# A norm's factors applied with tokens on partitions, and one recurrence's gates a slot sooner, in a two-block transformer kernel

## The reference, cut to what matters

```python
o = einsum('bhts,bhsv->bhtv', A, v)                          # 128 values per head and token
o = o * rsqrt(mean(o * o, axis=-1) + EPS) * norm_w           # a mean per head and token
o = o * silu(r)                                              # the gate
```

## Time and profile before

| | |
|---|---|
| median of 3 runs | 1113.66 us (1113.42 to 1113.71) |
| the profiled execution's own time | 1113.65 us |
| its span, first to last instruction | 1111.8 us |
| what lies around the span | 1.85 us |
| PE busy | 1097.7 us, 99% of the span |
| DVE busy, ACT busy | 750.7 us (68%), 608.6 us (55%) |
| mean granted TensorE clock | 0.998 of full speed |

### The profile page before, as it was taken

One profiled execution on the slowest core, in us unless ns is written; L12 is line 12 of the kernel. 1 busy time (PEld: TensorE's weight loads), 2 busy tenths in 40 slices (PEclk: granted clock), 3 DMA queues, 4 the chain that ended last, 5 costly groups with the idle time before them and its releaser, 6 DMA issues.

```text
span 1111.8 us, 22817 instructions
## 1 busy us (share of the span) xinstructions
PE 1097.7 (99%) x9532; PEld 1050.8 (95%) x9532; DVE 750.7 (68%) x980; ACT 608.6 (55%) x790; POOL 0.2 (0%) x4
## 2 busy tenths in 40 slices
PE   9999999999999999999999999999999999999997
PEld 8899999989999998999999999999999989999997
DVE  6355576677555555689969676866558657777776
ACT  6455456346444444687665555566555446545554
POOL 0000000000000000000000000000000000000000
PEclk9999999999999999999999999999999999999999
DMA  8433344564555555344434443444444545555451
GB/s 308 177 134 139 119 169 169 177 221 146 187 190 189 189 189 182 121 152 153 167 127 140 153 150 141 152 152 152 161 180 152 190 152 174 191 187 189 186 189 39
DMA packets 27113, 184.42 MB, mean 166 GB/s; under 512 B 3080, under 2 KB 3608, under 8 KB 5400
## 3 DMA queue, kind: packets, MB, share of 16 engines
q1 hardware_dynamic: 26456, 181.38, 45.6%
q10 hardware_dynamic: 576, 1.85, 0.5%
HBM read 182.17 MB, written 1.05 MB: 165 GB/s over the span
## 4 chain that ended last, share of the span: by engine, by line
PE 53%; DVE 1%; ACT 1%; issue 1%; ACTq 0%
PE pp L306 41%; PE pm L1733 2%; PE pm L1734 2%; PE pm L1735 2%; PE pm L919 1%; PE pm L389 1%; PE pm L387 1%; PE pm L388 1%; PE pm L1574 1%; PE pm L780 1%; PE pm L787 0%; PE pm L1349 0%; PE pm L1381 0%; DVE P L1067 0%; DVE wlo L288 0%
## 5 line engine op out<-in xcount | busy, mean ns | idle before, releaser
L288 DVE TENSOR_TENSOR wlo<-raw,whi 128x2048 fp32r<-128x2048 f32 x169 | 386.7, 2291 | 188.1 <-ACT whi L281 184.1
L306 PE MATMUL pp<-XH,whi 128*128 128x256 f32 x1696 | 485.5, 286 | 0.9 <-DVE wlo L288 0.5
L306 PE MATMUL pp<-XH,wlo 128*128 128x256 f32 x1696 | 481.3, 284 | 0.0
L306 PE MATMUL pp<-XL,whi 128*128 128x256 f32 x1696 | 481.3, 284 | 0.0
L281 ACT ACTIVATE whi<-raw 128x2048 fp32r<-128x2048 f32 x169 | 322.0, 1909 | 57.1 <-PE pp L306 33.8
L306 PEld LDWEIGHTS pp<-XH,whi 128*128 128x128 f32 x1696 | 326.0, 192 | 5.8 <-issue 2.4
L306 PEld LDWEIGHTS pp<-XL,whi 128*128 128x128 f32 x1696 | 326.1, 192 | 0.7
L306 PEld LDWEIGHTS pp<-XH,wlo 128*128 128x128 f32 x1696 | 326.1, 192 | 0.0
L1787 ACT ACTIVATE Y<-P 128x256 fp32r<-128x256 f32 x44 | 18.4, 418 | 132.6 <-DVE P L1820 132.6
L306 PE MATMUL pp<-Y,whi 128*128 128x256 f32 x480 | 86.9, 283 | 0.0
L306 PEld LDWEIGHTS pp<-Y,whi 128*128 128x128 f32 x480 | 75.2, 192 | 0.0
(11 more groups left out here) (321 smaller groups left out, 1300.1 us busy)
## 6 DMA issues: line engine op xcount, KB each, us to landing
raw<-stream SPq DMA_DIRECT2D x169, 1024.0 KB, 4.8
P<-gains ACTq DMA_DIRECT2D x3, 512.0 KB, 3.8
X<-xt SPq DMA_DIRECT2D x2, 512.0 KB, 4.3
raw<-stream SPq DMA_DIRECT2D x2, 512.0 KB, 6.7
out<-P SPq DMA_DIRECT2D x4, 256.0 KB, 2.3
C<-consts SPq DMA_DIRECT2D x1, 345.5 KB, 11.5
P<-rows_w ACTq DMA_DIRECT2D x1, 272.0 KB, 3.4
U<-poolw SPq DMA_DIRECT2D x1, 256.0 KB, 10.5
```

What stands on the lines that cost most here:

```text
L288: dve.tensor_tensor(wlo[:, slot, :], raw[:, slot, :], whi[:, slot, :].bitcast(F32), ALU.subtract).then_inc(lo_ready, 1)
L306: done = pe.matmul(dst, a, b, start=first and n == 0, stop=last and n == 2, **kw)
```

## The change

The outputs are made with the scores as the stationary operand, so tokens lie on partitions and each head's 128 channels along the row. The sum of squares is then a reduction along the row on DVE, and the eight factors are a column each, multiplied in by DVE while it takes `o` out of PSUM. Eight transposes on PE turn the scaled outputs back to channels on partitions, and one DVE instruction multiplies them by gain and gate. The `token_sum` and `spread_columns` matmuls, ACT's copy of `o` and the rounding of the columns go. PE has its two slots together (`st.go(2)`), ahead of the transposes. Besides, DVE's gates of r = 0 are queued one slot sooner.

```diff
 # gated_pe
-        o = [pm[:, 1024 + h * 256:1280 + h * 256] for h in range(4)]
+        o = [[pm[:, 1024 + u * 512 + h * 128:1152 + u * 512 + h * 128] for h in range(4)] for u in range(2)]
         for h in range(4):
-            pe.matmul(o[h][:, 128:256], g["v"](0, h), a_words(g, h)[:, 128:256], start=h % 2 == 0, ...)
+            pe.matmul(o[1][h], a_words(g, h)[:, 128:256], g["v"](0, h), start=h == 0, ...)
...
-        st.go(1)
-        pe.wait_ge(S("gated_squares"), r + 1)
+        st.go(2)
+        pe.wait_ge(S("gated_o_scaled"), r + 1)
         for h in range(4):
             for u in range(2):
-                i = token_sum(pe, bank(2)[:, 2 * h + u:2 * h + u + 1], HF[:, 4 + h, :], u)
-        i.then_inc(S("gated_sums"), 1)
-        st.go(1)
-        pe.wait_ge(S("gated_rsqrt"), r + 1)
-        pe.wait_ge(S("ident_rounded"), 1)
-        for h in range(4):
-            i = spread_columns(pe, bank(3 + h // 2)[:, (h % 2) * 256:(h % 2) * 256 + 256], (2 * h, 2 * h + 1))
-        i.then_inc(S("gated_norm_spread"), 1)
+                i = pe.transpose(bank(3 + h // 2)[:, (h % 2) * 256 + u * 128:(h % 2) * 256 + u * 128 + 128],
+                                 words(g["o"], u * 512 + h * 128, 128), ident)
+        i.then_inc(S("gated_o_turned"), 1)
 # gated_act
-        act.activation(P[:, g["o"]:g["o"] + 4, :], pm[:, 1024:2048]..., ACT.Copy).then_inc(S("gated_o_copied"), 1)
         act.activation(HF[:, 4:8, :], pm[:, 1024:2048]..., ACT.Square).then_inc(S("gated_squares"), 1)
...
-        act.activation(SC[:, 72:80], bank(2)[:, 0:8], ACT.Sqrt, bias=eps4, scale=4.0 / 128)
+        act.activation(SC[:, 72:80], SC[:, 72:80], ACT.Sqrt, bias=eps4, scale=4.0 / 128)
...
-            act.wait_ge(S("gated_rsqrt"), 3)
+            act.wait_ge(S("gated_o_scaled"), 3)
 # gated_dve
-        link(dve, dve.scalar_tensor_tensor(GD(g), GD(g), 1.0, P[:, g["r"]:g["r"] + 4, :], ALU.add, ALU.mult))
-        dve.wait_ge(S("gated_o_copied"), r + 1)
-        o = P[:, g["o"]:g["o"] + 4, :]
-        link(dve, dve.scalar_tensor_tensor(o, o, col(g["gain"]), GD(g), ALU.mult, ALU.mult))
+        gate, o = P[:, g["r"]:g["r"] + 4, :], P[:, g["o"]:g["o"] + 4, :]
+        link(dve, dve.scalar_tensor_tensor(gate, GD(g), 1.0, gate, ALU.add, ALU.mult))
         if r == 1:
             differences(0, gated(2))
+        by_head = lambda ap: ap.rearrange("p (n d) -> p n d", n=8)
+        dve.wait_ge(S("gated_squares"), r + 1)
+        dve.tensor_reduce(SC[:, 72:80], by_head(HF[:, 4:8, :]...), AX.X, ALU.add).then_inc(S("gated_sums"), 1)
         st.go(1)
         dve.wait_ge(S("gated_rms"), r + 1)
         link(dve, dve.reciprocal(SC[:, 80:88], SC[:, 72:80]))
-        round_columns(dve, SC[:, 80:88]).then_inc(S("gated_rsqrt"), 1)
+        dve.tensor_tensor(by_head(words(g["o"], 0, 1024)), by_head(pm[:, 1024:2048]),
+                          SC[:, 80:88].unsqueeze(2).to_broadcast([128, 8, 128]), ALU.mult).then_inc(S("gated_o_scaled"), 1)
         st.go(1)
...
-        dve.wait_ge(S("gated_norm_spread"), r + 1)
-        dve.tensor_tensor(o, o, pm[:, 1536:2560]..., ALU.mult).then_inc(S("gated_y_ready"), 1)
+        dve.wait_ge(S("gated_o_turned"), r + 1)
+        dve.scalar_tensor_tensor(o, pm[:, 1536:2560]..., col(g["gain"]), gate, ALU.mult, ALU.mult)
 # VectorE's queue, first stage
         gate_lo(dve, G1W[:, :], KT * 16, 1)
-        st.go(4)
+        st.go(3)
         gated_gates_dve(dve, 0)
         st.go(1)
         gated_decay_dve(dve, 0, slice(0, 2))
```

More of the change, by code:

```diff
@@ L925, in gated_pe @@
         wait_evac(pe, VALUES[r])
-        o = [pm[:, 1024 + h * 256:1280 + h * 256] for h in range(4)]
+        o = [[pm[:, 1024 + u * 512 + h * 128:1152 + u * 512 + h * 128] for h in range(4)] for u in range(2)]
         for h in range(4):
-            pe.matmul(o[h][:, 128:256], g["v"](0, h), a_words(g, h)[:, 128:256], start=h % 2 == 0, stop=False, skip_group_check=True)
+            pe.matmul(o[1][h], a_words(g, h)[:, 128:256], g["v"](0, h), start=h == 0, stop=False, skip_group_check=True)
         taken_scores(pe, r, 3)
@@ L931, in gated_pe @@
         for h in range(4):
-            pe.matmul(o[h][:, 0:128], g["v"](0, h), a_words(g, h)[:, 0:128], start=False, stop=True, skip_group_check=True)
-            i = pe.matmul(o[h][:, 128:256], g["v"](1, h), a_words(g, h)[:, 256:384], start=False, stop=True, skip_group_check=True)
+            pe.matmul(o[0][h], a_words(g, h)[:, 0:128], g["v"](0, h), start=h == 0, stop=True, skip_group_check=True)
+            i = pe.matmul(o[1][h], a_words(g, h)[:, 256:384], g["v"](1, h), start=False, stop=True, skip_group_check=True)
         i.then_inc(S("gated_o_ready"), 1)
-        st.go(1)
-        pe.wait_ge(S("gated_squares"), r + 1)
+        st.go(2)
+        pe.wait_ge(S("gated_o_scaled"), r + 1)
         for h in range(4):
             for u in range(2):
-                i = token_sum(pe, bank(2)[:, 2 * h + u:2 * h + u + 1], HF[:, 4 + h, :], u)
-        i.then_inc(S("gated_sums"), 1)
-        st.go(1)
-        pe.wait_ge(S("gated_rsqrt"), r + 1)
-        pe.wait_ge(S("ident_rounded"), 1)
-        for h in range(4):
-            i = spread_columns(pe, bank(3 + h // 2)[:, (h % 2) * 256:(h % 2) * 256 + 256], (2 * h, 2 * h + 1))
-        i.then_inc(S("gated_norm_spread"), 1)
+                i = pe.transpose(bank(3 + h // 2)[:, (h % 2) * 256 + u * 128:(h % 2) * 256 + u * 128 + 128],
+                                 words(g["o"], u * 512 + h * 128, 128), ident)
+        i.then_inc(S("gated_o_turned"), 1)
     def gated_logits_act(act):
@@ L1016, in gated_act @@
         act.wait_ge(S("gated_o_ready"), r + 1)
-        act.activation(P[:, g["o"]:g["o"] + 4, :], pm[:, 1024:2048].rearrange("p (a t) -> p a t", a=4), ACT.Copy)\
-           .then_inc(S("gated_o_copied"), 1)
         act.activation(HF[:, 4:8, :], pm[:, 1024:2048].rearrange("p (a t) -> p a t", a=4), ACT.Square)\
@@ L1023, in gated_act @@
         act.wait_ge(S("gated_sums"), r + 1)
-        act.activation(SC[:, 72:80], bank(2)[:, 0:8], ACT.Sqrt, bias=eps4, scale=4.0 / 128).then_inc(S("gated_rms"), 1)
+        act.activation(SC[:, 72:80], SC[:, 72:80], ACT.Sqrt, bias=eps4, scale=4.0 / 128).then_inc(S("gated_rms"), 1)
         st.go(1)
@@ L1129, in gated_dve @@
         dve.wait_ge(S("gated_r_tanh"), r + 1)
-        link(dve, dve.scalar_tensor_tensor(GD(g), GD(g), 1.0, P[:, g["r"]:g["r"] + 4, :], ALU.add, ALU.mult))
-        dve.wait_ge(S("gated_o_copied"), r + 1)
-        o = P[:, g["o"]:g["o"] + 4, :]
-        link(dve, dve.scalar_tensor_tensor(o, o, col(g["gain"]), GD(g), ALU.mult, ALU.mult))
+        gate, o = P[:, g["r"]:g["r"] + 4, :], P[:, g["o"]:g["o"] + 4, :]
+        link(dve, dve.scalar_tensor_tensor(gate, GD(g), 1.0, gate, ALU.add, ALU.mult))
         if r == 1:
             differences(0, gated(2))
+        by_head = lambda ap: ap.rearrange("p (n d) -> p n d", n=8)
+        dve.wait_ge(S("gated_squares"), r + 1)
+        dve.tensor_reduce(SC[:, 72:80], by_head(HF[:, 4:8, :].rearrange("p a t -> p (a t)")), AX.X, ALU.add).then_inc(S("gated_sums"), 1)
         st.go(1)
@@ L1139, in gated_dve @@
         link(dve, dve.reciprocal(SC[:, 80:88], SC[:, 72:80]))
-        round_columns(dve, SC[:, 80:88]).then_inc(S("gated_rsqrt"), 1)
+        dve.tensor_tensor(by_head(words(g["o"], 0, 1024)), by_head(pm[:, 1024:2048]), SC[:, 80:88].unsqueeze(2).to_broadcast([128, 8, 128]),
+                          ALU.mult).then_inc(S("gated_o_scaled"), 1)
         st.go(1)
@@ L1146, in gated_dve @@
                 dve.scalar_tensor_tensor(x, HF[:, 4 * b:4 * b + 4, :], 1.0, x, ALU.add, ALU.mult).then_inc(S("lm_silu"), 1)
-        dve.wait_ge(S("gated_norm_spread"), r + 1)
-        dve.tensor_tensor(o, o, pm[:, 1536:2560].rearrange("p (a t) -> p a t", a=4), ALU.mult).then_inc(S("gated_y_ready"), 1)
+        dve.wait_ge(S("gated_o_turned"), r + 1)
+        dve.scalar_tensor_tensor(o, pm[:, 1536:2560].rearrange("p (a t) -> p a t", a=4), col(g["gain"]), gate, ALU.mult, ALU.mult)\
+           .then_inc(S("gated_y_ready"), 1)
         if r != 1:
```

## The result

| | before | changed |
|---|---|---|
| median, first timing | 1113.66 us | 1102.82 us (1102.72 to 1102.86, 4 executions) |
| span of the profiled execution | 1111.8 us | 1101.0 us |
| ratio to the kernel before | | 0.9903, 95% interval 0.9886 to 0.9920 |

The changed kernel is 10.84 us faster; 11.4 were forecast (1102.3 us, range 1101.0 to 1104.8). The page of the changed kernel has the same balance as before: PE loses 72 matmuls and 10.6 us of busy time, and stays at 99%.

A forecast was written before the change was run, and what follows sets the result against it. PE, busy 99% of the span, was taken as the bound, so only its shorter queue or fewer waits help: 3.9 + 2.7 + 2.7 + 2.1 = 11.4 us off, forecast 1102.3 us, range 1101.0 to 1104.8.

The forecast's parts named there:

- gates a slot sooner: wait and clock: First scores of r = 0: PE's 2.45 us wait goes and 1.4 us of slow matmuls come back, 3.9 us.
- r = 0, PE's work behind the outputs: Sums and spreading go, eight transposes come: 9.37 us becomes one slot of 5.76 plus 0.93, gain 2.7 us.
- r = 1: Same pattern and durations behind the outputs of r = 1 as at r = 0: another 2.7 us.
- r = 2, limited by the chain on ACT and DVE: Ahead of L1363 the evacuation behind DVE's last multiplication holds PE some 0.9 us: gain 2.1 us instead of 2.7.
- the clock: First scores and levels of r = 0: without the pause no cause for the clock to fall, 1.4 us back.
- The upper end of 1.7: Highest price of each group of eight transposes, if each costs a two-part float32 matmul; gain at r = 0 then 1.9 us.
- No wait for DVE: Ahead of the transposes: scaled outputs ready 4.6 us before PE asks, 3.3 at the least; rival that they wait, 3%.
- The chain at r = 2: L281 starts near 636.15, 7.15 us to the gatings' end, last multiplication 643.3, next PE stage 649.4: gain 2.1 us.

The follow-up runs named there:

- the gates alone: The kernel before with only DVE's gates of r = 0 queued a slot sooner, old norm kept: 1109.48 us median over 7 executions.
- the norm alone: The changed kernel with the gates of r = 0 back in their old place: 1106.78, 1106.77, 1105.45 and 1105.28 us.
- the evacuation first: The changed kernel with, at r = 2, the last slot's evacuation queued ahead of the norm's last multiplication on ACT and DVE: 1101.36 us, again 1101.40.
- the run with four reductions: The changed kernel with DVE's reduction made four times in each recurrence: 1105.00, 1104.94, 1103.50 and 1103.43 us.
- one slot ahead of the transposes: The changed kernel with the transposes one slot sooner, one of PE's two slots ahead of them and one behind: 1105.32 us.

## Why the prediction was right, step by step

| step | forecast | measured |
|---|---|---|
| gates a slot sooner: wait and clock | 3.9 us | 4.0 by the gates alone (against the upper level); 4.0 from the traces |
| r = 0, PE's work behind the outputs | 2.7 | 2.64 |
| r = 1 | 2.7 | 2.62 |
| r = 2, limited by the chain on ACT and DVE | 2.1 | 1.78 |
| start of the kernel | none | 0.27 lost |
| sum | 11.4 | 10.8 |

The traces' values are distances between the same points. For the gates it is the start of the first level's matmuls, 61.96 before and 58.24 after: 3.72 sooner, although the first slot starts 0.27 later, so 4.0.

```profile
61.96 0.71 PE L908 MATMUL pm<-HF 64*128 64x128 f32 x8
```

```profile
58.24 0.71 PE L908 MATMUL pm<-HF 64*128 64x128 f32 x8
```

At r = 0 it is the distance from L1017 or L1012 to the attention's first matmul. At r = 1 and r = 2 it is the one from the first L932, among the outputs, to what follows the slots and the norm: the scores of r = 2 (L919), and `mlstm_pe`. Before, then after:

```profile
555.71 0.46 PE L932 MATMUL pm<-U,P 128*128 128x128 f32 x2 [0.42 <-ACT U L1014]
...
572.67 0.76 PE L919 MATMUL pm<-P,U 128*32 128x32 f32 x64
...
628.39 0.46 PE L932 MATMUL pm<-U,P 128*128 128x128 f32 x2 [0.42 <-ACT U L1014]
```

```profile
549.22 0.46 PE L932 MATMUL pm<-P,U 128*128 128x128 f32 x2 [0.42 <-ACT U L1009]
...
563.56 0.76 PE L919 MATMUL pm<-P,U 128*32 128x32 f32 x64
...
619.28 0.46 PE L932 MATMUL pm<-P,U 128*128 128x128 f32 x2 [0.42 <-ACT U L1009]
```

That is 16.96 and 14.34 us at r = 1, and with `mlstm_pe` at 651.48 and 640.59, 23.09 and 21.31 at r = 2. All of them sum to 10.8, the difference of the spans.

**The gates.** Every time in the chain came out within 0.3 us of the forecast, with the later start: decays done at 48.8 (48.6 forecast), first scores without a wait. The step that the prediction took as certain and that is not is the clock: a stretch at 0.50 follows the wait in most executions of the kernel before, not in all. The forecast was made against a median that lies on the upper level, so the sum held. The changed kernel's time does not depend on this, but the gain does: against the lower level it is some 9.3 us. That all four executions of the kernel before in the first timing lay on the upper level, as 9 of the 26 later ones did not, is luck.

**PE's work.** From the first transpose to what follows the eight it is 0.97 us at r = 0 and r = 1 and 0.79 at r = 2 (0.93 forecast), and doubling them added 0.9. The upper end of 1.7 is excluded.

**No wait for DVE.** Reduction 1.22 us (1.64 at most was allowed), scaling with a broadcast operand 1.22 as the plain one, 4.65 us of room (4.6 forecast). One slot less made PE wait, and 3.7 us more of DVE's work at r = 0 and r = 1 did not.

**The chain at r = 2.** The mechanism was as forecast, and the sign of it is shown twice: the transposes doubled there cost nothing, and the evacuation moved ahead of the chain removes the pause. The term was mis-sized by 0.3 us. From L281's start to L1141's end it took 7.16 us (7.15 forecast) and from L1143 to L1359 6.07 (6.08), but L281 began 0.55 us behind the end of PE's slot (632.65 - 5.76 = 626.89), where I had put 0.15. Of these 0.40 us 0.08 came back, since L1143 starts that much before L1141 ends. At r = 0 and r = 1 the same instruction begins 0.26 behind the slot's end. At r = 2 it is 0.54 or 0.55 with the norm alone, with the doubled transposes, with the evacuation first and in the second trace of the changed kernel too, so it is no accident of one execution; why it is longer there stays open.

**What no step had.** The first slot starts 0.27 us later. The first block of the weight stream, by the start of ACT's first split of it, comes 0.2 to 0.4 us later than before in the six different kernels with the new norm, again so in the second traces of two of them, and less than 0.1 later with the gates alone. No experiment told why; it is left open.

## What to carry to other kernels

Where one engine is at 99%, price a change by the distances between instruction starts on that engine, and then ask of every step whose end it now exposes: here two thirds of the gain was matmuls removed, and one in three recurrences gave back 0.9 us because ACT's and DVE's queues had another order of urgency than PE. A result that the bound engine waits for (an evacuation) belongs ahead of one that it needs a stage later. Work moved onto an engine with room is free only as far as that room reaches, and the room is a number in the trace.

## What the runs showed of the hardware that I had not expected

A pause of PE does not always cost clock. Behind the 2.45 us wait of the kernel before, and behind the 2.03 us pause of the run with four reductions, the executions fall on two levels 1.4 to 1.5 us apart, which is what the half-clock stretch costs in the trace (1.4); the traces taken were of executions on the upper level, and show the stretch. That the lower level is the absence of the stretch is inferred from this equality, from the kernels without such a wait, which have one level, and from the mean granted clock of each execution: of the kernel before's 26 later executions it is 0.999 in all nine on the lower level, 0.997 or 0.998 in the sixteen on the upper one, and 0.996 in the one at 1114.62. No trace of a lower execution was taken, and what decides between the levels is not shown. Pauses of 1.0 to 1.16 us, in nine executions of the changed kernel and four with one slot ahead of the transposes, never showed a second level. Where the wait was removed, the spread went with it: 0.3 us over the gates' seven executions and 0.2 over the changed kernel's nine, against 2.8 over the kernel before's thirty.

A reduction over 8 x 128 elements took 1.22 us, as much as a two-operand instruction of the same length, and a scaling with a column broadcast along 128 elements the same 1.22.
